# Merge of gated branches: four products from PSUM first, in place in the gate's tile, then four additions

## The reference

```python
gates = jax.nn.sigmoid(gate_logits + b_gate[l]).reshape(bn, s, N_BRANCH, d)
merged = (gates[:, :, 0] * (y_a @ w_branch[l, 0])
          + gates[:, :, 1] * (y_b @ w_branch[l, 1])
          + gates[:, :, 2] * (y_c @ w_branch[l, 2]))
x = x + merged @ w_out[l]
```

## Time and profile before

| what | value |
|---|---|
| median of 3 runs | 1702.03 us (1699.03 to 1704.1) |
| the profiled execution, its own time | 1697.58 us |
| its span, first to last instruction | 1695.8 us (1.78 us lie around it) |
| TensorE matmul busy | 1619.6 us, 96% |
| VectorE busy | 1010.1 us, 60% |
| ScalarE busy | 729.2 us, 43% |
| GpSimd busy | 57.8 us, 3% |
| mean granted TensorE clock | 0.995 of full speed |
| products of line 1758 | 48, the first at 319.3 us in the span, the last at 1017.3 us |
| additions of line 1761 | 32, the first at 352.4 us, the last at 1018.0 us |

### The profile page before, as it was taken

How to read it: one execution, slowest core, us unless ns; L and a number is a source line. 1 busy time by engine, 2 the same in 40 slices (tenths; PEclk the granted TensorE clock), 3 DMA queues, 4 the chain that set the end, 5 groups by cost and what they waited for, 6 DMA issues and landing times.

```text
span 1695.8 us, 21496 instructions
## 1 busy us (share of the span) xinstructions
PE 1619.6 (96%) x8009; PEld 1321.2 (78%) x8009; DVE 1010.1 (60%) x2246; ACT 729.2 (43%) x1503; POOL 57.8 (3%) x80
## 2 busy tenths in 40 slices
PE   6999999999999999999999999999989999997999
PEld 6878777787777878777787877898767779985667
DVE  4597656444444397757443344576886564778663
ACT  4444443333234443543332424434456553344662
POOL 0000002000001000002000001000000010000000
PEclk9999999999999999999999999999999999999999
DMA  7332121332323332112233323332112233211121
GB/s 219 96 87 75 39 61 53 97 98 90 98 89 89 92 92 87 51 50 63 75 96 91 100 87 112 94 84 68 61 33 68 81 87 99 81 49 45 38 75 62
DMA packets 80883, 136.23 MB, mean 80 GB/s; under 512 B 8190, under 2 KB 33420, under 8 KB 80780
## 3 DMA queue, kind: packets, MB, share of 16 engines
q1 hardware_dynamic: 77264, 129.48, 25.5%
q10 hardware_dynamic: 3516, 5.37, 1.1%
HBM read 132.74 MB, written 2.10 MB: 80 GB/s over the span
## 4 chain that ended last, share of the span: by engine, by line
PE 45%; DVE 13%; ACT 4%; issue 2%; POOL 0%; ACTq 0%; DVEq 0%
PE gemm_bank L695 34%; PE aux_bank L762 3%; PE aux_bank L791 3%; DVE w_lo L1340 2%; PE aux_bank L779 2%; DVE rope L1439 1%; ACT w_hi L1021 1%; DVE head_sums L1392 1%; DVE probs L1495 1%; ACT probs L1068 1%; DVE kT L1479 1%; PE aux_bank L750 1%; DVE probs L1507 1%; DVE product L1758 0%; ACT L1293 0%
## 5 line engine op out<-in xcount | busy, mean ns | idle before, releaser
L1021 ACT ACTIVATE w_hi<-raw 128x512 fp32r<-128x512 f32 (+3 forms) x524 | 305.5, 587 | 681.5 <-PE gemm_bank L695 680.1
L1340 DVE TENSOR_TENSOR w_lo<-raw,w_hi 128x512 fp32r<-128x512 f32 (+3 forms) x524 | 330.7, 636 | 445.0 <-ACT w_hi L1021 443.3
L695 PE MATMUL gemm_bank<-act_hi,w_hi 128*128 128x512 f32 x768 | 318.4, 415 | 14.9 <-DVE product L1758 3.8
L695 PE MATMUL gemm_bank<-act_hi,w_lo 128*128 128x512 f32 x768 | 300.8, 392 | 0.0
L695 PE MATMUL gemm_bank<-act_lo,w_hi 128*128 128x512 f32 x768 | 300.2, 391 | 0.0
L695 PE MATMUL gemm_bank<-w_hi,act_hi 128*128 128x384 f32 (+3 forms) x736 | 269.1, 366 | 6.5 <-DVE bq L1380 2.9
L695 PE MATMUL gemm_bank<-w_hi,act_lo 128*128 128x384 f32 (+3 forms) x736 | 257.4, 350 | 0.0
L695 PE MATMUL gemm_bank<-w_lo,act_hi 128*128 128x384 f32 (+3 forms) x736 | 257.4, 350 | 0.0
L695 PEld LDWEIGHTS gemm_bank<-act_hi,w_hi 128*128 128x128 f32 x768 | 144.6, 188 | 57.1 <-issue 12.7
L695 PEld LDWEIGHTS gemm_bank<-act_lo,w_hi 128*128 128x128 f32 x768 | 144.9, 189 | 31.1 <-issue 2.9
L695 PEld LDWEIGHTS gemm_bank<-act_hi,w_lo 128*128 128x128 f32 x768 | 144.5, 188 | 31.1
(11 more groups left out here) (289 smaller groups left out, 2133.7 us busy)
## 6 DMA issues: line engine op xcount, KB each, us to landing
raw<-in_w_in SPq DMA_DIRECT2D x104, 512.0 KB, 3.6
raw<-in_w_in SPq DMA_DIRECT2D x64, 384.0 KB, 3.3
raw<-in_w_out SPq DMA_DIRECT2D x32, 512.0 KB, 3.7
raw<-in_w_branch SPq DMA_DIRECT2D x24, 512.0 KB, 3.8
raw<-in_w_mem_kv SPq DMA_DIRECT2D x8, 512.0 KB, 3.7
raw<-in_w_in SPq DMA_DIRECT2D x16, 256.0 KB, 2.7
raw<-in_w_in SPq DMA_DIRECT2D x8, 416.0 KB, 4.9
x<-in_x SPq DMA_DIRECT2D x4, 512.0 KB, 5.2
```

Of the source, the lines that this page charges most:

```text
L695: last = pe.matmul(o, a, c, start=begin and n == 0, stop=end and n == 2)
L1021: act.activation(w_hi[:, s % RING, 0:n], raw[:, p % RAW, kk % PIECE, 0:n], ACT.Copy)\
L1340: dve.tensor_tensor(w_lo[:, s % RING, 0:n], raw[:, p % RAW, kk % PIECE, 0:n], w_hi[:, s % RING, 0:n].bitcast(F32), ALU.subtract).then_inc( ...
```

## The change

For i = 1 and 2 VectorE makes the four products one after the other, each written over the gate values that it reads, and then the four additions, which read the gate's tile. The tile `product` is gone. The additions of i = 1 count a new semaphore, `products_added`. `settle()` at the head of the merge and between the products goes away; for i = 2 there is one wait for the additions of (j, 1). On ScalarE, the sigmoid that overwrites a gate buffer waits for what was last to read it: for n = 2 and 5 the product of merge n - 2 as before, for n = 3 the additions of (0,1), for n = 4 the additions of (0,2).

```diff
--- before.py
+++ after.py
@@ -271,7 +271,6 @@
     squared = at("squared", [P, 2, NT, T], F32, Y + 32 * KB)
     merged = at("merged", [P, KD, T], F32, A)
     gate = at("gate", [P, 2, 4, T], F32, A + 16 * KB)
-    product = at("product", [P, 2, T], F32, A + 32 * KB)
@@ -414,6 +413,7 @@
     gate_ready = sem("gate_ready")
     merged_ready = sem("merged_ready")
+    products_added = sem("products_added")
@@ -1191,9 +1191,12 @@
                 split.through(gi)
                 for m in range(4):
                     wait_gemm_full(act, gi, m)
-                    if n >= 2:
-
-                        wait_gemm_read(act, gi_of(1, l, "branch", (n - 2) // 3, (n - 2) % 3), m)
+                    if n in (2, 5):
+                        wait_gemm_read(act, gi_of(1, l, "branch", (n - 2) // 3, 0), m)
+                    elif n == 3:
+                        act.wait_ge(products_added, 8 * l + 4)
+                    elif n == 4:
+                        act.wait_ge(merged_ready, KD * l + m + 1)
@@ -1747,22 +1750,19 @@
             split.through(g_gate)
             split.through(gi)
-            settle()
+            if i == 2:
+                dve.wait_ge(products_added, 8 * l + 4 * (j + 1))
             for m in range(4):
                 wait_gemm_read(dve, g_gate, m)
                 wait_gemm_full(dve, gi, m)
+                mine = gate[:, n % 2, m, :]
+                dst = merged[:, 4 * j + m, :] if i == 0 else mine
+                dve.tensor_tensor(dst, gemm_bank[m][:, :], mine, ALU.mult).then_inc(gemm_read[m], 1)
+            for m in range(4 if i else 0):
+                wait_gemm_read(dve, gi, m)
                 mm = merged[:, 4 * j + m, :]
-                dst = mm if i == 0 else product[:, m % 2, :]
-                if i and m >= 2:
-                    settle()
-                dve.tensor_tensor(dst, gemm_bank[m][:, :], gate[:, n % 2, m, :], ALU.mult).then_inc(gemm_read[m], 1)
-                if i:
-                    wait_gemm_read(dve, gi, m)
-                    ins = dve.tensor_tensor(mm, mm, product[:, m % 2, :], ALU.add)
-                    if i == 2:
-                        ins.then_inc(merged_ready, 1)
-                    else:
-                        mark(ins)
+                dve.tensor_tensor(mm, mm, gate[:, n % 2, m, :], ALU.add)\
+                   .then_inc(merged_ready if i == 2 else products_added, 1)
```

## The result

| | before | changed |
|---|---|---|
| median | 1700.53 us (1697.97 to 1704.1, 4 runs) | 1689.81 us (1688.14 to 1690.31, 4 runs) |
| ratio of the times, 95% interval | | 0.9934 (0.9912 to 0.9955) |
| span of the profiled execution | 1695.8 us | 1688.5 us |
| its mean granted clock | 0.995 | 0.993 |
| VectorE busy | 1010.1 us | 1005.9 us |

What follows compares the result with a forecast made beforehand. TensorE's stream was taken as the bound: 10.57 us lost at six places plus 0.6 at the two merges (0,1), 11.2 in all, so 1702.03 - 11.2 = 1690.8 us; range 1686 to 1698 us.

Steps and rivals of the forecast that it cites:

- the loss is at step 0 behind merges with additions: TensorE's first step behind such merges takes over 2.72 us; 10.57 us lost at six places, 0.40 at each (0,1).
- Four products first: At merges with i = 1 and 2, products ahead of additions free banks in time, as at (1,0); 11.2 us gained.
- The spare time of bank 0: At (0,2), bank 0 is free at 387.11 and wanted by TensorE at 387.62; 0.5 us to spare.
- In place costs nothing: On VectorE, a product written over the gate it reads takes no longer; neither cost nor gain.
- The rival of a second pass: VectorE's product over its own gate is slower; at twice 0.684 us each, 4.4 us slower, 1706.4 us; chance 0.04.
- p: Time a VectorE product over its own gate takes, in place of 0.60 us; at 1.25 TensorE stands as long as now.
- The waits and the count: At the merges, without `settle()`, VectorE's eight instructions take about 4.95 us instead of 5.39; off the path.
- same count, same time: Rival: VectorE's eight instructions at a merge hold TensorE as long as now; nothing gained, 1702 us; chance 0.06.
- handed back at "out": Rival: TensorE stands at step 3 of "out" instead of step 0; at most 3.2 us back, 1694.0 us; chance 0.10.
- Merge (0,0) keeps its wait: Merges (0,0) and (1,0) keep their instructions and gain nothing; TensorE's waits stay at (0,0).
- The span near 1684.6 us: Sign in the changed profile that the forecast holds: the span of the profiled execution near 1684.6 us.
- shifts as a whole: What follows the merges (update of x, norms, attention) starts from TensorE's results and only moves earlier.

Runs made afterwards that it cites:

- the kernel with the products in place alone: Changed kernel with each addition put back behind its product, products still over the gate and no `settle()`; 1700.3 us over 10 runs, ratio 1.0001 to the kernel before.
- the kernel of the row products: Changed kernel with the last two row products of the third branch moved behind merge (0,0); medians 1688.44 and 1686.46 us, ratios 0.9924 and 0.9921 to the kernel before.

## Why the prediction was right

- *TensorE's stream is the bound, and the loss is at step 0 behind merges with additions.* Right: 10.57 us at six places and 0.8 at two were read, 11.36 in all; 0.21 are left, where I left 0.2.
- *Four products first take all of it, as at (1,0).* Right: with the waits of the changed kernel, alternating products and additions lose 9.90 us and four products first 0.21, in place or not. The spare time of bank 0 was taken too large: the prediction has 0.5 us, counted from the end of the product, and measured were 0.36.
- *In place costs nothing.* Right: 681 ns, 2.48 us for four. The rival of a second pass, with p = 1.37 us, falls; p is 0.60 (2.48 less 0.68, over three distances).
- *The waits and the count.* VectorE was to need 4.95 us for eight; it is 389.55 + 2.49 - 387.16 = 4.88. The rival "same count, same time" falls. The Trainium skill, page "VectorE: DVE Perf Modes", section "Rules for kernel authors", has the count of operations matter and not the semaphores. The trace does not agree. At the same count the kernel with the products in place alone lost the `settle()` between addition and product, and at (1,1) a pair went from 1.55 us (0.73 and 0.82) to 1.33 (0.72 and 0.61); moving the additions, at the same count again, then took the rest.
- *Nothing is handed back at "out".* Right. VectorE's and TensorE's rows at the start of "out", against the earlier trace rows:

```profile
489.88 2.49 DVE L1771 TENSOR_TENSOR merged_lo<-merged,merged_hi 128x512 fp32r<-128x512 f32 x4
492.29 1.89 DVE L1343 TENSOR_TENSOR w_lo<-raw,w_hi 128x512 fp32r<-128x512 f32 x3
...
494.43 0.39 PE L695 MATMUL gemm_bank<-w_hi,merged_hi 128*128 128x512 f32 x1
```

  The first `w_lo` is done at 492.98 (492.29 + 0.69) and step 3 starts at 494.43, 8.16 us behind step 0, so without a wait (three steps of 2.72 are 8.16); 1.45 us of slack, 1.3 worked out.
- *Merge (0,0) keeps its wait.* Right, 0.97 us ahead of step 0 in each layer; it was two row products that stood in front, not something that the change could reach.
- *The span near 1684.6 us.* This was off by 3.9 us: 1688.5. The step that failed is that what follows "shifts as a whole". The work did, but the granted clock outside the merges did not stay: the rest took 1334.4 us in this profile against 1330.5 in the first of the kernel before. With three profiles of each it is 1331.6 and 1333.5 us on average, a difference within what one kernel's profiles show.

The gain hit because over several executions this evens out: 11.15 us taken from TensorE's waits, 10.7 us in the medians, and 11.4 twice more. That the time itself came within 1.0 us of the 1690.8 forecast is in part luck: the forecast started from 1702.03 us, the median of three executions, and later medians of the same kernel were 1699.63, 1699.68 and 1700.84 us.

## What to carry to other kernels

Where one engine drains banks that another wants back at a fixed pace, compare the pace of release with the pace of demand, not busy times: VectorE was 60% busy and still held TensorE, since work that TensorE did not wait for stood between two releases. Put everything that frees a bank first and the rest behind it, and look for a place in the same kernel that already has that form: it gives the gain before the edit is made. Then measure the slack that is left (here 0.4 us), because beyond it each delay ahead of the first release is paid in full.

## What was not expected of the hardware

- A few microseconds of total time hang on the granted clock in stretches where TensorE pauses. Two profiles of the kernel before differed by 3.5 us in span, two of the kernel of the row products by 6.6, with merges equal within 0.1 us. A gain of 1.5 to 2 us can be shown in the stretch where it arises and not in the total.
- A VectorE operation of 128x512 float32 follows the one before after 0.60 to 0.61 us if its waits are already met, and after 0.72 to 0.73 if it waits for that one's completion, or 0.82 behind the wait for everything marked; the duration shown is 0.68 to 0.69 each time.
